# One 8 KB gather per expert row, each weighted sum right behind its dot, and tile 1's projections in quarters

## The reference

```python
def peer(xn, wq, subkeys, u, v):
    ...
        q = jnp.einsum('nd,dk->nk', xb, wq).reshape(P_TOK_BLOCK, P_HEADS, 2, P_DKEY // 2)
        s = jnp.einsum('nhcd,hckd->nhck', q, subkeys).astype(jnp.float32)
        sv, si = lax.top_k(s, P_TOPK)
        ...
        fv, fi = lax.top_k(cand, P_TOPK)
        eidx = jnp.take_along_axis(cidx, fi, axis=-1)
        g = jax.nn.softmax(fv, axis=-1)
        ue = u[eidx]
        ve = v[eidx]
        act = jax.nn.gelu(jnp.einsum('nd,nhkd->nhk', xb, ue).astype(jnp.float32), approximate=False)
        return jnp.einsum('nhk,nhkd->nd', (g * act).astype(ve.dtype), ve)
```

## Time and profile before

| | |
|---|---|
| median of 3 runs | 1261.18 us (1260.83 to 1262.43) |
| span of the profiled execution | 1192.3 us |
| the runs' median beyond that span | 68.9 us |
| TensorE busy | 1048.0 us (88%) |
| VectorE busy | 793.0 us (67%) |
| GpSimd busy | 735.0 us (62%) |
| ScalarE busy | 362.9 us (30%) |
| DMA moved | 468.12 MB, 393 GB/s over the span |
| gathers | 384 of u, 384 of v |

### The profile page before, as it was taken

How to read it: one execution, slowest core, us unless ns; L and a number is a source line. 1 busy time by engine, 2 the same in 40 slices (tenths; PEclk the granted TensorE clock), 3 DMA queues, 4 the chain that set the end, 5 groups by cost and what they waited for, 6 DMA issues and landing times.

```text
span 1192.3 us, 11355 instructions
## 1 busy us (share of the span) xinstructions
PE 1048.0 (88%) x3311; PEld 511.3 (43%) x3311; DVE 793.0 (67%) x1943; ACT 362.9 (30%) x853; POOL 735.0 (62%) x774
## 2 busy tenths in 40 slices
PE   9999999999868987898979899997888888778886
PEld 4767565664325543433535355442223222223332
DVE  2639986998765588998546575784674664773344
ACT  2535235324131343333322333321212212222120
POOL 0004565566655677777746566776776777776774
PEclk9999999999989999999989999999999999999999
DMA  9967999999999999999999999999999999999997
GB/s 373 411 231 252 410 412 412 360 398 409 406 401 409 384 368 390 409 409 408 415 408 408 410 408 404 406 408 414 409 409 410 408 410 409 409 409 376 410 409 303
DMA packets 125628, 468.12 MB, mean 393 GB/s; under 512 B 14072, under 2 KB 17152, under 8 KB 123392
## 3 DMA queue, kind: packets, MB, share of 16 engines
q0 software_dynamic: 110592, 402.70, 85.4%
q1 hardware_dynamic: 14976, 64.70, 13.6%
HBM read 462.86 MB, written 4.42 MB: 392 GB/s over the span
## 4 chain that ended last, share of the span: by engine, by line
DMA 26%; PE 20%; POOL 14%; DVE 8%; issue 6%; ACT 0%; POOLq 0%; DVEq 0%; ACTq 0%
DMA UV<-in_p_v,EIDX 18%; PE PSUM L1978 14%; POOL UV L579 8%; DMA UV<-in_p_u,EIDX 7%; POOL UV L564 6%; DVE UV L1475 3%; PE PSUM L1757 2%; PE PSUM L1731 1%; PE PSUM L1700 1%; PE PSUM L1774 1%; POOL UV L572 1%; DVE SEL L213 0%; DVE SEL L219 0%; DVE UV L215 0%; DVE SEL L211 0%
## 5 line engine op out<-in xcount | busy, mean ns | idle before, releaser
L1978 PE MATMUL PSUM<-UV,DIAG 128*128 128x512 f32 x1500 | 727.2, 617 | 124.9 <-DMA UV<-in_p_v,EIDX 119.2
L1475 DVE CUSTOM_DVE_ANT_0 UV<-UV,PSUM 128x1024 f32<-128x1024 f32 x384 | 462.9, 1218 | 269.7 <-DMA UV<-in_p_u,EIDX 265.8
L564 POOL DMA_INDIRECT UV<-in_p_u,EIDX x384 | 367.2, 956 | 254.5 <-issue 97.1
L1978 PEld LDWEIGHTS PSUM<-UV,DIAG 128*128 128x128 f32 x1500 | 267.3, 192 | 523.4 <-DMA UV<-in_p_v,EIDX 293.6
L579 POOL DMA_INDIRECT UV<-in_p_v,EIDX x376 | 358.6, 954 | 186.4 <-PE PSUM L1978 104.4
L1001 ACT ACTIVATE DIAG<-CST,WGT 128x128 f32<-128x128 f32 x375 | 149.1, 401 | 697.0 <-PE PSUM L1978 696.3
L1558 PE MATMUL PSUM<-WR,XW 128*128 128x512 f32 (+1 forms) x128 | 50.6, 554 | 0.1
L1567 PE MATMUL PSUM<-XW,WR 128*128 128x256 f32 x192 | 42.3, 379 | 0.0
L1567 PEld LDWEIGHTS PSUM<-XW,WR 128*128 128x128 f32 x192 | 36.5, 190 | 6.8 <-issue 1.9
L1558 PEld LDWEIGHTS PSUM<-WR,XW 128*128 128x128 f32 x128 | 24.2, 190 | 25.3 <-issue 22.7
L211 DVE MAX8 SEL<-UV 128x8 f32<-128x128 f32 (+1 forms) x71 | 21.5, 330 | 15.6 <-ACT UV L604 12.6
(11 more groups left out here) (292 smaller groups left out, 818.7 us busy)
## 6 DMA issues: line engine op xcount, KB each, us to landing
WR<-in_w_o SPq DMA_DIRECT2D x13, 512.0 KB, 8.2
UV<-in_p_u,EIDX POOLq DMA_INDIRECT x384, 10.5
UV<-in_p_v,EIDX POOLq DMA_INDIRECT x384, 10.5
WR<-in_p_wq SPq DMA_DIRECT2D x10, 512.0 KB, 7.4
UV<-in_w_o SPq DMA_DIRECT2D x2, 2048.0 KB, 14.6
UV<-in_p_wq SPq DMA_DIRECT2D x2, 2048.0 KB, 9.7
WR<-in_w_B SPq DMA_DIRECT2D x2, 2048.0 KB, 8.1
UV<-in_w_B SPq DMA_DIRECT2D x4, 512.0 KB, 6.5
```

Source lines behind the costliest of these rows:

```text
L564: nc.gpsimd.indirect_dma_start(UBUF[n % RU], None, a["p_u"], bass.IndirectOffsetOnAxis(EIDX[:, n:n + 1], 0)).then_inc(u_got[n % RU], 16)
L1475: v.tensor_tensor_reduce(out=row, in0=row, in1=XNP, scale=1.0, scalar=0.0, op0=ALU.mult, op1=ALU.add, accum_out=DOTS[:, i % 2, s:s + 1]).t ...
L1978: ins = mm(bank[6 + k][:, :], DIAG[:, m % ND, :], VBUF[m % RV][:, k * 512:(k + 1) * 512], start=False, stop=m % SLOTS == SLOTS - 1 or m == ...
```

## The change

**One gather, one ring.** The host lays u and v side by side (`p_uv`, 8 KB for an expert). One indirect DMA brings both halves of row n into one of `RING` = 7 places. The place is free again when TensorE has added the row (`row_summed`), and gather n waits for row n - 7. The lag is gone: `LAGS`, `slot_at`, `FINE` and `BORROWED` go away.

**The chain of a row.** After the dot of row n (`dot_done`), ScalarE does a GELU of one column, a copy of one column scaled with the gate (the gate is divided by its sum on VectorE beforehand, `gate_ready`), and the DIAG. TensorE adds the row at once. `DOTS`, `GELU` and `WGT` are rings of 32 columns. TensorE adds 382 rows, VectorE the last two (`ADDED`). The sum of tile 0 no longer starts with h; h is added at its end, so that the sum may start early.

**Tile 1's front.** TensorE's slots are now rows of its own sum, from the first. A projection unit is cut in four parts at `UNIT_SLOT` + 0, 1, 3 and 4, a quarter after a row. All slots of the trunks, the choices (106 and 221), the gates and the weight loads are written anew: the softmax of tile 1 comes ahead of the last four units, its recurrence behind them.

**Tables.** ScalarE's program has 107 table loads where it had 66. Of them 48 stand at the one-column GELU.

```diff
...
-RU, RV, ND = 8, 6, 6
...
+RING, ND, NW = 7, 6, 32
...
-UNIT_SLOT = [2, 5, 8, 12, 16, 20, 24, 27, 31, 34, 42, 45, 49, 57]
+UNIT_SLOT = [1, 7, 13, 19, 25, 30, 35, 42, 50, 56, 64, 70, 78, 84]
...
+ADDED = [382, 383]
+SUMMED = [n for n in range(HEADS * PK) if n not in ADDED]
...
-            def gather_u(n):
+            def gather(n):
                 if n % PK == 0:
                     pool.wait_ge(heads_chosen, n // PK + 1 + (n > 0))
                 elif n == 8:
                     pool.wait_ge(heads_chosen, 2)
-                if n >= RU:
-                    pool.wait_ge(u_free, n - RU + 1)
+                if n == 3:
+                    take(pool, ("qq", 0, 3))
+                elif n == 5:
+                    take(pool, ("qq", 0, 7))
+                elif n >= RING:
+                    pool.wait_ge(row_summed, done_before(n - RING, SUMMED) + 1)
                 nc.gpsimd.indirect_dma_start(
-                    UBUF[n % RU], None, a["p_u"], bass.IndirectOffsetOnAxis(EIDX[:, n:n + 1], 0)
-                ).then_inc(u_got[n % RU], 16)
-
-            def gather_v(n):
-                if n in BORROWED:
-                    k = BORROWED[n]
-                    pool.wait_ge(u_free, k + 1)
-                    nc.gpsimd.indirect_dma_start(
-                        UBUF[k % RU], None, a["p_v"], bass.IndirectOffsetOnAxis(EIDX[:, n:n + 1], 0)
-                    ).then_inc(u_got[k % RU], 16)
-                    return
-                m = n if n < ALONE else ALONE + (n - ALONE) // 2
-                if m >= RV:
-                    pool.wait_ge(v_free, m - RV + 1)
-                nc.gpsimd.indirect_dma_start(
-                    VBUF[m % RV], None, a["p_v"], bass.IndirectOffsetOnAxis(EIDX[:, n:n + 1], 0)
-                ).then_inc(v_got[m % RV], 16)
-
+                    ROWS[place_of(n)], None, a["p_uv"], bass.IndirectOffsetOnAxis(EIDX[:, n:n + 1], 0)
+                ).then_inc(row_got[place_of(n)], 16)
 
             take(pool, ("wo", 0, 1))
-            asked = 0
             for n in range(HEADS * PK):
-
-                ahead = 5 if n < 72 else 1
-                while asked < min(HEADS * PK, slot_at(max(0, n - RV)) + min(n, RV) + ahead):
-                    if asked == 4:
-                        take(pool, ("qq", 0, 3))
-                    gather_u(asked)
-                    asked += 1
-                if n == 0:
-                    take(pool, ("qq", 0, 7))
-                gather_v(n)
+                gather(n)
...
-            def weigh(m):
-                n = v_row(m)
-                i, s = n // PK, n % PK
-                if i < FINE:
-                    if s == 0:
-                        act.wait_ge(wgt_done, i + 1)
-                elif n >= ALONE or s % PART == 0:
-                    act.wait_ge(wgt_done, FINE + (n - FINE * PK) // PART + 1)
+
+            def weigh(n):
+                i, at = n // PK, slice(n % NW, n % NW + 1)
+                act.wait_ge(dot_done, n + 1)
+                own.done(nc.scalar.activation(GELU[:, at], DOTS[:, at], ACT.Gelu))
+                if n % PK == 0:
+                    act.wait_ge(gate_ready, i + 1)
+                weight = nc.scalar.activation(WGT[:, at], GELU[:, at], ACT.Copy, scale=GATE[:, n:n + 1])
+                if n in ADDED:
+                    weight.then_inc(wgt_done, 1)
+                    return
+                own.done(weight)
+                m = done_before(n, SUMMED)
                 if m >= ND:
-                    act.wait_ge(v_free, m - ND + 1)
-                nc.scalar.activation(DIAG[:, m % ND, :], IDENT, ACT.Copy, scale=WGT[:, i % NW, s:s + 1]).then_inc(diag_ready, 1)
-                if s == ND - 1 and i and i % PH == 0:
-                    read_y(i // PH - 1)
-                if m >= ND:
-                    fronts(slot_at(n - ND))
+                    act.wait_ge(row_summed, m - ND + 1)
+                nc.scalar.activation(DIAG[:, m % ND, :], IDENT, ACT.Copy, scale=WGT[:, at]).then_inc(diag_ready, 1)
...
+            for n in range(HEADS * PK):
+                weigh(n)
+                if n and n % SLOTS == 0:
+                    read_y(n // SLOTS - 1)
+                fronts(n)
...
+            def add(n, out, before):
+                row, weight = VROW[place_of(n)], WGT[:, n % NW:n % NW + 1]
+                dve.wait_ge(wgt_done, done_before(n, ADDED) + 1)
+                own.done(v.scalar_tensor_tensor(out=out, in0=row, scalar=weight, in1=before, op0=ALU.mult, op1=ALU.add))
...
-                row = UBUF[n % RU]
+                row = UROW[place_of(n)]
                 if n and n % SLOTS == 0:
                     rows_for_dots(n // SLOTS)
-                dve.wait_ge(u_got[n % RU], 16 * (n // RU + 1))
+                if n == 383:
+
+                    dve.wait_ge(row_summed, len(SUMMED))
+                    add(382, X[2], PSUM[:, 6 * 512:8 * 512])
+                dve.wait_ge(row_got[place_of(n)], 16 * (n // RING + 1))
                 v.tensor_tensor_reduce(out=row, in0=row, in1=XNP, scale=1.0, scalar=0.0,
-                                       op0=ALU.mult, op1=ALU.add, accum_out=DOTS[:, i % 2, s:s + 1]).then_inc(u_free, 1)
+                                       op0=ALU.mult, op1=ALU.add, accum_out=DOTS[:, n % NW:n % NW + 1]).then_inc(dot_done, 1)
...
+            def two_heads(name, w, k, part):
+                pb = start(name) if part == 0 else bank[PLACE[name][0]]
+                at, h = part // 2, 2 * k + part // 2
+                for c in range(part % 2 * 4, part % 2 * 4 + 4):
+                    ins = mm(pb[:, at * 256:(at + 1) * 256], w[:, c, h * P:(h + 1) * P], XNT12[:, :, c, :], start=c == 0, stop=c == KC - 1)
+                if part == 3:
+                    end(ins, name)
...
             def unit(n):
                 chunk, k = UNITS[n]
-                w = later_weights(chunk)
                 name = unit_name(chunk, k)
-                if chunk[0] == "B" or chunk == "AI":
-                    rows_of(name, XNT12[:, k - 1], w)
-                else:
-                    channels_of(name, XNT12, w, (2 * k, 2 * k + 1))
+                for part, slot in enumerate((0, 1, 3, 4)):
+                    yield UNIT_SLOT[n] + slot
+                    w = later_weights(chunk)
+                    if chunk[0] == "B" or chunk == "AI":
+                        rows_of(name, XNT12[:, k - 1], w, 2 * part, 2 * part + 2)
+                    else:
+                        two_heads(name, w, k, part)
...
+            for n in range(HEADS * PK):
+                t = n // SLOTS
+                if n and n % SLOTS == 0:
                     pe.wait_ge(y_ready, 2 * t)
-                for n in range(2):
-                    mm(bank[6 + n][:, :], IDENT, X[t][:, n * 512:(n + 1) * 512], start=True, stop=False)
-                for m in range(t * SLOTS, min((t + 1) * SLOTS, SUMS)):
-                    pe.wait_ge(v_got[m % RV], 16 * (m // RV + 1))
+                    add_h(t, True)
+                if n in SUMMED:
+                    m = done_before(n, SUMMED)
                     pe.wait_ge(diag_ready, m + 1)
+                    ends = n == 2 * SLOTS - 1 or n == SUMMED[-1]
                     for k in range(2):
-                        ins = mm(bank[6 + k][:, :], DIAG[:, m % ND, :], VBUF[m % RV][:, k * 512:(k + 1) * 512],
-                                 start=False, stop=m % SLOTS == SLOTS - 1 or m == SUMS - 1)
-                        if k == 0 and m % SLOTS == SLOTS - 1:
+                        ins = mm(bank[6 + k][:, :], DIAG[:, m % ND, :], VROW[place_of(n)][:, k * 512:(k + 1) * 512],
+                                 start=n == 0, stop=ends)
+                        if n == 2 * SLOTS - 1 and k == 0:
                             ins.then_inc(y_full, 1)
-                    ins.then_inc(v_free, 1)
-                    trunks(slot_at(m))
+                    ins.then_inc(row_summed, 1)
+                if n == SLOTS - 1:
+                    add_h(0, False)
+                trunks(n)
...
-    o["p_u"], o["p_v"] = i["p_u"][0], i["p_v"][0]
+    o["p_uv"] = np.concatenate([i["p_u"][0], i["p_v"][0]], axis=1)
...
```

More of the change, by code:

```diff
@@ L963, in _ @@
             square_h(0)
-            def gelus():
-                for i in range(FINE):
-                    yield i * PK + PK + 1
-                    gelu(i)
-                for n in range(FINE * PK, HEADS * PK, PART):
-                    yield n + 2
-                    gelu(n // PK, n % PK, n % PK + PART)
-            first, trunks, gated, gelued = in_slots(choices(0)), in_slots(trunk()), in_slots(gates()), in_slots(gelus())
+            first, trunks, gated = in_slots(choices(0)), in_slots(trunk()), in_slots(gates())
             first(CHOICES[0] + 6)
@@ L1812, in trunk @@
                         turned(1, kv, g)
-                yield 77
-                new_state(1)
-                yield 78
-                values(1)
-                for c in MIXED[1][0:4]:
-                    yield (80, 81, 83, 84)[c]
-                    mixed(1, c)
```

(22 more changed lines are left out.)

373 lines of the change are left out of this document (155 added, 218 removed).

## The result

The changed kernel takes 1273.37 us (median of 8 runs, 1263.1 to 1283.87), the kernel before beside it 1262.54 us (8 runs, 1259.61 to 1265.23): ratio 1.007, 95% interval 1.0043 to 1.0096. (One of its eight runs, the 1283.87 that was also profiled, counts as slow and is not in the ratio, which takes the median of the other seven, 1271.66.) The forecast was 1268.7 us, in a range of 1236 to 1297, and slower.

What follows compares the result with a forecast made beforehand. TensorE and DMA were taken as both full until 486 us, DMA alone after. Row 112 at 491.6, gathers 655.7 and other transfers 30.7 made 1178.0; waits 16, tail 5.8: span 1199.8, plus 68.9: 1268.7 us, range 1236 to 1297.

Steps and rivals of the forecast that it cites:

- The start of the rows: First row sum: after gates end at 116.1, table load, GELU, weight and DIAG put it at 118.2 us.
- the rival of a costly switch: Rival, chance 0.02: each table load on the chain in tile 1 and the softmax costs 1.3 us more, giving 1313.
- TensorE's stage: Rows 0 to 111, limited by TensorE: 334.4 us of work plus 39 of waits, row 112 due at 491.6 us.
- tile 1's keys: Wait in rows 0 to 111: ScalarE's copies, squares, root and table loads leave TensorE idle for 7.5 us.
- Cut in quarters they cost the same: Tile 1's projections in rows 0 to 111: cutting units in four leaves their TensorE time at 93.1 us.
- the price of a sum: TensorE, rows 0 to 111: 0.429 us a pass, 1.716 a row, 192.2 us for 112 rows.
- the 41 us for the weights and the rest: DMA's transfers other than gathers beside rows 0 to 111: 147.6 MB less 130.9 of gathers, 41 us of DMA's 316.
- Rows 112 to 255: Part of rows 112 to 383, taken as DMA's: 2.456 us a row at 427 GB/s, plus other transfers and waits.
- the ring's slack: Rows 112 to 383: seven rows last 17.2 us against a place's 12.6, so only hold-ups over 4.6 us stop the queue.
- The term "16": Waits behind row 112: 8 us for tile 2's softmax, 8 for its keys, root, choices and queries; bounds 4 and 30.
- my third rival: Rival, chance 0.09: ring too short, gates with a choice use up its slack, 2 us lost in 17 heads, 1299.
- The runs' median stands 68.9 over the span: Step from span to timed runs: 68.9 us added to the span of 1199.8, unaffected by the change, giving 1268.7.

Runs made afterwards that it cites:

- a_again: The changed kernel, unchanged, run again for a second profile: 1270.55 us, ratio 1.0628 to the kernel before, which took 1195.49 us there.
- gate: The changed kernel with the gates' Exp replaced by a GELU (wrong result), 44 of 107 table loads gone: 1263.86 us, ratio 1.0586 to the kernel before.
- b_third: The kernel before, unchanged, profiled once more: 1194.6 us at a span of 1192.8.
- ring6: The changed kernel with six ring places instead of seven: 1289.79 us, ratio 1.0221 to the kernel before at 1264.38 us.
- lag13: The kernel before with a constant lead of 13 rows instead of 28 to 50, and FINE 0: 1263.66 us, ratio 1.0006 to the kernel before.
- shift1: The changed kernel with ScalarE's trunk work and gates one row later than TensorE's and VectorE's slots: 1263.66 us, ratio 1.0 to the kernel before.
- shift12: The changed kernel with ScalarE's trunk work and gates one row later, two from row 145 on: 1271.98 us, ratio 1.0062 to the kernel before.
- split: The changed kernel with two 4 KB gathers per row into the same seven places: 1282.8 us, ratio 1.0736 to the kernel before.
- b_fill: The kernel before with a one-byte GpSimd memset ahead of each of its 768 gathers: 1195.95 us, ratio 1.0 to the kernel before.

## Why the prediction was right, and where it wasn't

**The start of the rows: right.** TensorE's and ScalarE's timelines of a_again, at the first weight:

```profile
118.50 6.17 PE L1911 MATMUL PSUM<-UV,DIAG 128*128 128x512 f32 x8 [6.15 <-ACT DIAG L958]
```

```profile
113.72 1.28 ACT L752 ACT_TABLE_LOAD   x1
115.01 0.31 ACT L752 ACTIVATE GATE<-SEL,SMALL 128x16 f32<-128x16 f32 x1
...
115.89 0.19 ACT L752 ACTIVATION_READ_ACCUMULATOR GATE<-SEL,SMALL 128x1 f32 x1
116.10 1.28 ACT L947 ACT_TABLE_LOAD   x1
117.39 0.20 ACT L947 ACTIVATE GELU<-DOTS 128x1 f32<-128x1 f32 x1
117.63 0.30 ACT L950 ACTIVATE WGT<-GELU,GATE 128x1 f32<-128x1 f32 x1
117.95 0.40 ACT L958 ACTIVATE DIAG<-CST,WGT 128x128 f32<-128x128 f32 x1
```

The first sum starts at 118.5; predicted was 118.2. The loads end and the next instruction stands 0.01 us behind them, so the rival of a costly switch is out here too: the 2.66 us that the Trainium skill, "ScalarE: Activation LUTs", section "What ACT_TABLE_LOAD costs", gives for a switch are 1.28 in this trace, and gate shows that even these are mostly hidden.

**TensorE's stage: the waits right, the work 12 us short.** 385.4 us from the first sum to that of row 112, of which TensorE was busy for 346.0, so idle for 39.4; predicted were 39. That is no luck, since the stops agree one by one: tile 1's keys took 6.7 us (7.5 in the prediction), the other stream's squares 2.0 (1.9), the dots with Ln and gates 6.3 (6.0), the softmax numerators 6.3 (5.7), and a unit copied with another table 1.25, four times (1.0 to 1.1, six times). The work was put at 334.4: it came out 11.6 more. Taking each pass up to the start of the next instruction, the trace has 209.1 us of sums, 94.1 of projections and 42.8 of all else; the prediction had 192.2, 93.1 and 49.1. So "Cut in quarters they cost the same" holds to 1 us, the other work was put 6 too high, and the step that failed is the price of a sum: 0.429 us a pass, from twelve passes back to back, where it is 0.467 (209.1 / 448). That is not for rows standing alone now, as the groups of sums before (112.4 to 486 us) and now (118.5 to 504 us) are nearly alike:

```profile
L1978 PE MATMUL PSUM<-UV,DIAG 128*128 128x512 f32 x395 | 191.0, 622 | 27.6 <-DMA UV<-in_p_v,EIDX 27.1
L1911 PE MATMUL PSUM<-UV,DIAG 128*128 128x512 f32 x449 | 222.3, 625 | 45.5 <-ACT DIAG L958 45.5
```

The passes have a mean of 622 ns before and 625 now, and up to the start of the next instruction the 395 of before take 184.3 us, 0.467 each as well. So the price was there to be read in the stage itself. (The busy time of a group counts the end of its last pass although the next group has begun; the groups of this stage add up to some 372 us, where TensorE was busy for 346.0.) The granted clock in this stage was 0.96, and 0.97 before. One slip on DMA's side changed nothing: the 41 us for the weights and the rest subtract all gathers until 486 us, of which 4.19 MB lie ahead of 112.4.

**Rows 112 to 255: the step that failed.** Predicted were 144 x 2.456 = 354, 31 for the other transfers and 16 of waits: 400. It took 442. The same 442 us in three parts, first the changed kernel, then the kernel before (b_third):

```profile
504.00:640.00 136.00, 108.20 (x326) 54.39 (x325) 87.52 (x207) 71.72 (x191) 39.95 (x42) 0.92 0.88 341
640.00:800.00 160.00, 129.31 (x393) 61.92 (x392) 106.04 (x250) 90.04 (x227) 50.13 (x53) 0.95 0.94 373
800.00:946.00 146.00, 136.41 (x468) 69.34 (x469) 97.76 (x261) 68.97 (x204) 47.76 (x50) 0.98 0.98 393
```

```profile
504.00:640.00 136.00, 117.76 (x367) 57.03 (x368) 92.01 (x226) 39.49 (x104) 91.61 (x95) 0.97 1.03 410
640.00:800.00 160.00, 150.90 (x506) 74.19 (x504) 110.19 (x278) 48.26 (x118) 108.87 (x116) 1.00 1.02 403
800.00:946.00 146.00, 115.67 (x238) 41.88 (x236) 89.36 (x217) 35.31 (x82) 104.78 (x110) 0.98 1.03 410
```

Before, DMA ran at 410, 403 and 410 GB/s and TensorE had its bursts beside it (150.9 of 160 us in the middle part). Now neither is full until 800 us, and from there both nearly are (TensorE busy for 136.4 of 146, DMA share 0.98). TensorE waited in this stage for:

```profile
PE PSUM L1911 <- ACT DIAG L958: 60.1, 34, 5.4
PE PSUM L1690 <- DMA WR<-in_p_wq: 4.0, 1, 4.0
PE PSUM L1897 <- ACT X L966: 4.0, 2, 2.7
```

I had summed this stage as if DMA were its only limit and put the ring's slack against single stops. But TensorE has 374 us of work in it and DMA some 385 of transfers, nearly the same.

The trace also tells what TensorE waited for behind the DIAG. Of the waits of over 0.3 us ahead of a row's first pass, 59 us in all, 40 us (21 rows) are for rows whose dot had been done for over 1 us when ScalarE began their GELU, 16 us (7 rows) for rows that had landed over 1 us before VectorE began their dot, and only 3 us (2 rows) for rows that had just landed. So this is the wait that the prediction had counted for tile 1's stage, ScalarE standing in the chain of each row in program order, and VectorE with it. The failed step is that it was put at 16 us for tile 2, as if the ring's slack and the DMA queue covered the rest. That the ring of seven is too short to carry DMA over these stops is argued from this: ring6 has one place less and took 7 us more in this stage, no more than two executions of one kernel differ by, and no run had a longer ring. One such stop, tile 2's keys, on all engines:

```profile
546.37 1.98 PE L1911 MATMUL PSUM<-UV,DIAG 128*128 128x512 f32 x4
546.53 0.77 ACT L571 ACTIVATE UV<-PSUM,SMALL 128x128 f32<-128x128 f32 x2 [1.70 <-PE PSUM L1707]
...
547.33 0.84 ACT L623 ACTIVATE WR<-ZB 128x768 f32<-128x768 f32 x1
...
548.21 0.95 DVE L1005 TENSOR_REDUCE SMALL<-WR 128x12 f32<-128x768 f32 x1 [5.66 <-ACT WR L623]
...
549.24 1.28 ACT L626 ACT_TABLE_LOAD   x1 [1.06 <-DVE SMALL L1005]
...
550.76 1.28 ACT L947 ACT_TABLE_LOAD   x1
...
552.62 0.40 ACT L958 ACTIVATE DIAG<-CST,WGT 128x128 f32<-128x128 f32 x1
...
553.07 3.27 PE L1911 MATMUL PSUM<-UV,DIAG 128*128 128x512 f32 x4 [4.72 <-ACT DIAG L958]
553.48 1.22 DVE L1423 CUSTOM_DVE_ANT_0 UV<-UV,PSUM 128x1024 f32<-128x1024 f32 x1
```

TensorE is idle for 4.72 us, VectorE begins no dot between 541.31 and 553.48 (it waited 5.66 us for ScalarE's squares and then normed the keys), and GpSimd's next gather waits for the sum. So the whole chain of the rows stands still together. It is the same piece of work that I priced at 7.5 us for tile 1; for tile 2 I gave it a part of 8 us. The term "16" measured 58 (442.3 less 353.7 and 30.7), or 54 by what was moved: the queue carried 163.55 MB in this stage, 388.5 us at 421 GB/s.

**Rows 256 to 383: 16 us over.** Predicted were 308, measured 323.8. The 129.16 MB of gathers in it take 306.8 us at 421 GB/s and 302.5 at 427, so 4 us are the rate. The 3.30 MB of other transfers, which the 400 above already hold, are 8, and the tail was 5.8 us, as predicted. That leaves 3.4 us for all stops. TensorE's waits there are:

```profile
PE PSUM L1911 <- ACT DIAG L958: 70.7, 89, 3.4
```

Most of these by number, 62 rows with 32 us, are for a row that has just landed, and the others cost next to nothing, since the queue is full beside them. So the gates and choices of tile 2, my third rival, cost at most 3.4 us here.

Sum: 11.6 + 0.4 + 42 + 16 = 70, which is 1270.0 - 1199.8.

**From the span to the runs: wrong, and the reason that the number fits.** "The runs' median stands 68.9 over the span" was read as a constant that the change leaves alone. It is 2 to 3 us. The other 67 us are what the kernel before loses on some chips, and the changed kernel does not lose them. The two errors, 70 too few for the change and 67 too many for the surroundings, cancel. That is luck: neither has to do with the other in the prediction.

Why does the kernel before lose them? No profile of it exists from such a chip. Of lag13, which is nearly the same kernel and took the same time as it there, one does. Windows of lag13 and then of shift1, an 8 KB kernel, on the same chip:

```profile
900.00:1100.00 200.00, 145.75 (x289) 51.55 (x287) 124.53 (x325) 42.50 (x110) 130.78 (x138) 0.96 0.97 371
1100.00:1240.00 140.00, 99.95 (x192) 34.77 (x193) 72.56 (x152) 25.57 (x70) 93.14 (x99) 0.95 0.97 369
```

```profile
900.00:1100.00 200.00, 163.83 (x383) 66.40 (x381) 138.49 (x348) 84.60 (x258) 74.99 (x79) 0.97 1.01 419
1100.00:1240.00 140.00, 107.62 (x223) 39.33 (x223) 89.39 (x202) 58.84 (x183) 52.67 (x56) 0.99 1.01 420
```

With two gathers of 4 KB a row it moves 371 and 369 GB/s, with one of 8 KB 419 and 420, as on the quick chips. (That 8 KB is what differs is not shown: the kernels differ in more.) From 950 to 1080 us lag13's DMA in 40 slices:

```profile
GB/s 257 281 342 415 410 411 408 406 412 250 289 279 376 416 416 402 410 410 410 303 330 382 258 270 398 418 406 412 412 406 411 263 271 272 382 412 411 410 410 408
```

Most slices have 400 to 418, and five times there are two or three slices of 250 to 345 in a row. The engines of lag13 at one of them ("remote" is an end of a wait for which the view names no instruction):

```profile
1050.08 1.98 PE L1978 MATMUL PSUM<-UV,DIAG 128*128 128x512 f32 x4 [0.58 <-DMA UV<-in_p_v,EIDX]
1051.63 0.18 DVE L1261 CAST SEL<-SEL 128x32 f32<-128x32 uint32 x1 [2.71 <-remote]
1051.63 0.40 ACT L1001 ACTIVATE DIAG<-CST,WGT 128x128 f32<-128x128 f32 x1 [9.40 <-remote]
...
1051.86 1.09 POOL L579 DMA_INDIRECT UV<-in_p_v,EIDX  x1 [4.33 <-remote]
```

VectorE, ScalarE and GpSimd stand still and go on together, within 0.23 us, while TensorE adds its rows at the usual pace. The gather and the DIAG both wait for `v_free`, which TensorE's sums count up. Sums ended at 1044.39, 1046.95 and 1049.51; the trace records three counts of `v_free` at 1051.61, 1051.67 and 1051.75. So the work was done, and the count of the semaphore came late; VectorE waited for a count of its own in the same way. In the quick execution b_third every sum has its count within 0.02 us of its end; in lag13 only 274 counts are recorded for 375 sums, so a part is missing from its trace altogether. GpSimd's waits with such an end in lag13 are

```profile
POOL UV L579 <- remote: 56.6, 22, 4.4
```

and none of the kernel before's three traces has one. On lag13's chip the traces of the 8 KB kernels (ring6, shift1, shift12) don't show it either: 382 or 383 counts for 382 sums, at most one of them late, and at most 5 of the counts of 384 dots. So what the kernel before loses on such chips is, as far as lag13 stands for it, late counts, and these 56.6 us are near the 67 us.

Why they come late there stays open. The kernel before has two gathers a row, each with 16 counts, and the changed one has one; whether it is their number or the size of the packets that matters wasn't told apart, as split ran on a quick chip. That GpSimd, at 1.24 us a gather against DMA's 1.28, has no room to catch up was only argued: b_fill ran on a quick chip and didn't move the pace.

So: slower in both kinds of sets, by 0.7% where the kernel before is held up and by 6% where it isn't. Of the mechanism, the waits in TensorE's stage and a modest gain from packets (12 us by split) are as forecast; the waits behind row 112 were more than three times as large as I made them, and the price of a sum was too low.

## What to carry to other kernels

Where a chain of three engines stands behind each row, count the stops of the middle engine in every stage, and not only in the one where TensorE is full: here they were 40 us of TensorE's waits in the first stage and 40 in the second, for which the prediction had 39 and, with all else, 16. Take the price of an instruction from the stage that it is used in, and not from its best stretch. Where two engines have about the same work over a stage, it should help to sum it in stretches as long as the ring between them and to take the slower of the two in each; that is a proposal, which no run here tried. Compare stages of two traces before explaining a difference of their times: shift12's lay ahead of its edit. And compare the span of a profile with the timed runs before using both: a difference of 5% is not an overhead but another execution, and asks for a second profile.
